# A sample tile's outputs and its 32 state updates moved from behind a chunked scan into it

## What is computed

```python
def gla_block(S, q, k, v, log_a):
    b = jnp.cumsum(log_a, axis=1)
    qf = q * jnp.exp(b); kf = k * jnp.exp(-b)
    inter = jnp.einsum('bchk,bhkv->bchv', qf, S)
    att = tril(jnp.einsum('bihk,bjhk->bhij', qf, kf))
    intra = jnp.einsum('bhij,bjhv->bihv', att, v)
    k_tail = k * jnp.exp(b[:, -1:] - b)
    S_new = S * jnp.exp(b[:, -1])[..., None] + jnp.einsum('bjhk,bjhv->bhkv', k_tail, v)
    return S_new, inter + intra

def gla_output(o, r, g_norm, w_o):
    return (rms_norm(o, g_norm) * silu(r)) @ w_o
```

## Time and profile before

| | |
|---|---|
| median of 3 runs | 2890.35 us |
| the profiled execution | 2889.26 us |
| its span, first to last instruction | 2886.8 us |
| PE busy (share of the span) | 2791.4 us (97%) |
| DVE, ACT, POOL busy | 1168.9, 866.4, 1236.5 us |
| mean granted TensorE clock | 0.989 |

### The profile page before, as it was taken

How to read it: one execution, slowest core, us unless ns; L and a number is a source line. 1 busy time by engine, 2 the same in 40 slices (tenths; PEclk the granted TensorE clock), 3 DMA queues, 4 the chain that set the end, 5 groups by cost and what they waited for, 6 DMA issues and landing times.

```text
span 2886.8 us, 39210 instructions
## 1 busy us (share of the span) xinstructions
PE 2791.4 (97%) x15484; PEld 2420.7 (84%) x15484; DVE 1168.9 (40%) x2079; ACT 866.4 (30%) x1513; POOL 1236.5 (43%) x654
## 2 busy tenths in 40 slices
PE   7999999999999999999999988899999999999997
PEld 7977757799889988997788867777798899989986
DVE  2153156452322233246544178855463322232245
ACT  2053242231222223222211056653141222222221
POOL 1211210343776567634212122133252775677645
PEclk9999999999999999999999999999999999999999
DMA  4111216110210221031444333476111201221021
GB/s 134 52 37 44 91 64 226 37 52 30 59 36 22 58 58 44 15 95 37 128 135 143 123 134 107 168 291 236 44 53 36 55 8 54 58 58 31 27 73 66
DMA packets 197372, 232.26 MB, mean 80 GB/s; under 512 B 8944, under 2 KB 141808, under 8 KB 195200
## 3 DMA queue, kind: packets, MB, share of 16 engines
q1 hardware_dynamic: 197248, 230.54, 24.8%
HBM read 184.90 MB, written 45.61 MB: 80 GB/s over the span
## 4 chain that ended last, share of the span: by engine, by line
PE 44%; DVE 4%; issue 1%; DMA 1%; ACT 1%; POOL 0%; SPq 0%; DVEq 0%; ACTq 0%
PE ps L1480 13%; PE ps L1498 12%; PE ps L1781 8%; PE ps L1668 3%; DVE stats L2513 1%; PE ps L1884 1%; PE ps L1751 1%; PE ps L1847 1%; PE ps L1918 1%; DMA o_scr<-oraw 1%; PE ps L1871 1%; PE ps L1470 1%; DVE stats L2226 1%; PE ps L1962 1%; ACT PR L1360 0%
## 5 line engine op out<-in xcount | busy, mean ns | idle before, releaser
L1480 PE MATMUL ps<-xt,wsplit 128*128 128x384 f32 x5184 | 908.2, 335 | 13.1 <-DVEq L2253 5.0
L1480 PEld LDWEIGHTS ps<-xt,wsplit 128*128 128x128 f32 x5184 | 900.8, 188 | 17.9 <-issue 7.1
L852 POOL TENSOR_TENSOR wsplit<-raw,wsplit 128x1024 fp32r<-128x1024 f32 x144 | 354.7, 2470 | 920.8 <-ACT wsplit L1072 843.1
L1498 PE MATMUL ps<-wsplit,xt 128*128 128x512 f32 x3024 | 707.0, 393 | 0.0
L1498 PEld LDWEIGHTS ps<-wsplit,xt 128*128 128x128 f32 x3024 | 564.8, 189 | 122.0 <-issue 6.5
L1781 PE MATMUL ps<-wsplit,HF 128*128 128x512 f32 x2016 | 468.6, 390 | 0.0
L1781 PEld LDWEIGHTS ps<-wsplit,HF 128*128 128x128 f32 x2016 | 377.3, 188 | 81.6 <-DVE x_res L2359 4.2
L2359 DVE TENSOR_TENSOR x_res<-x_res,ps 128x1024 f32<-128x1024 f32 x168 | 205.2, 1221 | 308.3 <-PE ps L1781 308.3
L2351 DVE TENSOR_SCALAR Hf<-ps 128x384 f32<-128x384 f32 x144 | 80.3, 558 | 499.1 <-PE ps L1480 498.4
L1278 ACT ACTIVATE Hf<-Hf 128x384 f32<-128x384 f32 x144 | 75.9, 527 | 428.1 <-DVE Hf L2351 428.1
L922 POOL TENSOR_TENSOR wsplit<-raw,wsplit 128x1024 fp32r<-128x1024 f32 x36 | 86.0, 2389 | 263.9 <-ACT wsplit L1255 263.9
(11 more groups left out here) (196 smaller groups left out, 2782.8 us busy)
## 6 DMA issues: line engine op xcount, KB each, us to landing
raw<-in_w_up SPq DMA_DIRECT2D x64, 512.0 KB, 5.5
raw<-in_w_down SPq DMA_DIRECT2D x64, 512.0 KB, 3.7
kq_scr<-kqst SPq DMA_DIRECT2D x64, 256.0 KB, 2.8
Kc<-in_cache_k SPq DMA_DIRECT2D x8, 2048.0 KB, 13.3
Vc<-in_cache_v SPq DMA_DIRECT2D x8, 2048.0 KB, 8.8
raw<-in_w_in_a SPq DMA_DIRECT2D x24, 512.0 KB, 3.7
out<-kvs SPq DMA_DIRECT2D x36, 256.0 KB, 2.2
raw<-in_w_kv SPq DMA_DIRECT2D x16, 512.0 KB, 4.4
```

What stands on the lines that cost most here:

```text
L852: nc.gpsimd.tensor_tensor(wsplit[:, slot, 1, :], raw[:, slot, :], wsplit[:, slot, 0, :].bitcast(F32), ALU.subtract).then_inc(lo_done, 1)
L1480: last = nc.tensor.matmul(ps[0:M, b, 0:GW], st, xt[:, c, k, ng * GW:(ng + 1) * GW], start=(k == 0 and i == 0), stop=(k == KT - 1 and i == 2))
L1498: last = nc.tensor.matmul(ps[:, u % 6, :], xt[:, a, 2 * j + k, tok:tok + P], wsplit[:, (g + j) % 4, c, k * 512:(k + 1) * 512], start=(j == ...
```

## The change

The sample tile becomes the third of nine "places" (`SMP = 2`): its transposes, scores, state reads and masked products are issued once, ahead of step 8 (`sample_outputs`). Its 32 state updates, called units, are spread over steps 8 to 31: a unit's product goes into columns 256 to 511 of bank 2 or 3, behind the step's key-value product into the same bank, and DVE updates the stream's state behind S1 or behind S0. Steps 8 to 31 have 1, 1, 2, 1, 1, 2, ... units: 16 steps have one (in bank 2), 8 have two. A copy of the sample tile's values is made on POOL (`vS`). The gate of tile 0 moves to step 8, that of tile 1 behind the last step. The states are written to HBM as their units come; the prompt's final state goes into the buffer of a stream's state that has been written out, and is stored from there.

```diff
+    def units_of(s):
+        behind = max(0, s - FIRST_UNIT)
+        n = SCAN_STEPS - FIRST_UNIT
+        return range(behind * UNITS // n, (behind + 1) * UNITS // n) if s >= FIRST_UNIT else range(0)
...
-        for t in range(2):
-            gates_back(t)
-        sp.wait_ge(state_updated, 2 * PT * H_A)
-        sp.dma_start(gla_prompt[0, 0].rearrange("h k v -> k h v"), S[:, 0]).then_inc(states_out, 16)
-        for t in range(2, 4):
+        for t in range(3):
             gates_back(t)
         for e in range(2):
             for j in range(STREAMS // 2):
-                sp.wait_ge(smp_updated, 4 * (2 * e + 1) + j + 1)
+                sp.wait_ge(smp_updated, 16 * e + 4 * j + 4)
...
+        sp.wait_ge(state_updated, 2 * PT * H_A)
+        sp.dma_start(gla_prompt[0, 0].rearrange("h k v -> k h v"), Ss[1][:, 0]).then_inc(odd_states_out, 16)
+        gates_back(3)
+        sp.wait_ge(scan_out, H_A * TILES)
...
             for c in range(2):
                 if s:
                     pe.wait_ge(state_updated, 2 * (s - 1) + c + 1)
-                nc.tensor.matmul(ps[:, 2 + c, 0:DV], kts[c * CH:(c + 1) * CH, s % 2, :],
-                                 vO[c * CH:(c + 1) * CH, t, h * DV:(h + 1) * DV],
-                                 start=True, stop=True).then_inc(scan_kv, 1)
+                if units_until(s, c):
+                    pe.wait_ge(smp_updated, units_until(s, c))
+                last = nc.tensor.matmul(ps[:, 2 + c, 0:DV], kts[c * CH:(c + 1) * CH, s % 2, :],
+                                        vO[c * CH:(c + 1) * CH, t, h * DV:(h + 1) * DV], start=True, stop=True)
+                for m in units_of(s)[c:c + 1]:
+                    e, j, hs_ = unit(m)
+                    last = nc.tensor.matmul(ps[:, 2 + c, DV:2 * DV], ktb[32 * j:32 * j + 32, e, hs_ * P:(hs_ + 1) * P],
+                                            vS[32 * j:32 * j + 32, hs_ * DV:(hs_ + 1) * DV], start=True, stop=True)
+                last.then_inc(scan_kv, 1)
...
         for s in range(steps):
+            if s == FIRST_UNIT:
+                sample_outputs()
+                pe.wait_ge(smp_blocks, 1)
             if s + 1 < steps:
                 scores(s + 1)
             outputs(s)
...
-        state_products(0, 0)
-        pe.wait_ge(smp_masked, 1)
...
-        state_products(0, 1)
-        state_products(1, 0)
-        state_products(1, 1)
-        pe.wait_ge(smp_updated, 2 * STREAMS)
-        pe.wait_ge(scan_normed, 2 * TILES)
...
+            if (t, half) == (0, 0):
+                pe.wait_ge(keys_by_token, SCAN_STEPS)
+                pe.wait_ge(scores_masked, SCAN_STEPS)
+                pe.wait_ge(state_updated, 2 * SCAN_STEPS)
+                pe.wait_ge(smp_updated, UNITS)
...
+            units = units_of(s)
+            if s == FIRST_UNIT:
+                dve.wait_ge(smp_state_out, 1)
+            for m in units[0:1]:
+                state_unit(m, 2)
             dve.wait_ge(scan_kv, 2 * s + 2)
...
+            to = Ss[1][:, 0, h, :] if t == PT - 1 else S[:, 0, h, :]
+            nc.vector.scalar_tensor_tensor(to, S[:, 1, h, :], elast[:, h, 2 * t + 1:2 * t + 2],
                                            ps[:, 3, 0:DV], ALU.mult, ALU.add).then_inc(state_updated, 1)
+            for m in units[1:2]:
+                state_unit(m, 3)
...
+            if s == FIRST_UNIT:
+                dve.wait_ge(smp_scores, 1)
...
+                gate(0)
...
+                if s == FIRST_UNIT + 2:
+                    normed(2 * SMP)
+                    normed(2 * SMP + 1)
...
-        mean_square(steps // 2 - 1)
-        normed(steps // 2 - 1)
...
-        gate(0)
+        mean_square(pair(steps // 2 - 1))
         gate(1)
```

More of the change, by code:

```diff
@@ L415, in sample_scores, with place_of, tile_at, scan_outs @@
         return ps[:, 2 * (w % 2):2 * (w % 2) + 2, :].rearrange("p a n -> p (a n)")[:, 0:512 + SEQ_S]
+    SMP = 2
+    SCAN_STEPS = PT * H_A
+    FIRST_UNIT = SMP * H_A
+    UNITS = 4 * STREAMS
+    def place_of(t):
+        return SMP if t == PT else t + (t >= SMP)
+    def tile_at(place):
+        return PT if place == SMP else place - (place > SMP)
+    def scan_outs(s):
+        return H_A * place_of(s // H_A) + s % H_A + 1
+    def units_of(s):
+        behind = max(0, s - FIRST_UNIT)
+        n = SCAN_STEPS - FIRST_UNIT
+        return range(behind * UNITS // n, (behind + 1) * UNITS // n) if s >= FIRST_UNIT else range(0)
+    def units_until(s, c):
+        return max([m + 1 for v in range(s) for m in units_of(v)[c:c + 1]], default=0)
+    def unit(m):
+        return m // 16, m // 4 % 4, m % 4
     PRODUCTS = ("k", "k", "q", "q", "v", "v")
@@ L1155, in squares @@
         def squares(p):
-            t, hp = p // 2, p % 2
-            act.wait_ge(scan_out, 4 * t + 2 * hp + 2)
+            place, hp = p // 2, p % 2
+            act.wait_ge(scan_out, 2 * p + 2)
             if p >= 4:
@@ L1173, in _ @@
         for s in range(steps):
+            if s == FIRST_UNIT:
+                act.wait_ge(smp_turned, 4)
+                for e in range(2):
+                    last = nc.scalar.mul(ktb[:, e, :], ps[:, 0, :], cst[:, C_SG + e:C_SG + e + 1])
+                last.then_inc(smp_blocks, 1)
             if s + 2 < steps:
@@ L1177, in _ @@
                 to_tokens(s + 1)
+            if s == FIRST_UNIT:
+                squares(2 * SMP)
+                squares(2 * SMP + 1)
             if s % 2 == 1:
[L1179 to L1194, removed]
+                squares(2 * place_of(s // H_A) + s // 2 % 2)
+        act.wait_ge(scan_out, H_A * TILES)
+        act.wait_ge(smp_updated, UNITS)
+        act.wait_ge(states_out, 16 * STREAMS // 2)
         for grp in range(NG):
@@ L1563, in outputs @@
             t, h = s // H_A, s % H_A
+            place = place_of(t)
             pe.wait_ge(keys_by_token, s + 1)
+            if s == FIRST_UNIT:
+                pe.wait_ge(smp_blocks, 1)
+                pe.wait_ge(smp_q_spread, 4)
             for c in range(2):
@@ L1590, in _ @@
             outputs(s)
[L1593 to L1628, removed]
@@ L1641, in _ @@
[L1641 to L1644 removed]
+        def gated_half(t, half):
+            if (t, half) == (0, 0):
[3 more added lines that the diff above has]
+                pe.wait_ge(smp_updated, UNITS)
+            if (t, half) == (1, 1):
+                pe.wait_ge(scan_normed, 2 * TILES)
```

106 lines of the change are left out of this document (63 added, 43 removed).

## The result

The changed kernel took **2974.17 us** (median of 4 runs, 2943.78 to 2976.41) against 2889.74 us of the kernel before: ratio 1.0265, interval 1.0198 to 1.0333, 2.7% slower. The forecast was 2908, with a range of 2897 to 2916: the direction was right, the size was not. The profiled execution took 2976.41 us, its span is 2974.5 us, the mean granted clock 0.964.

The account below looks back on a forecast made before the run. A DVE loop was taken to pace scan steps at 2.57 us, and DVE the work behind the scan. Terms 7.0 + 28.4 + 0.9 - 17.7 = +18.6 gave 2908 us, range 2897 to 2916.

Parts of the forecast that it names:

- Sample block, +7.0: Ahead of step 8: the sample tile's outputs hold up the scan on PE, 7.0 us more.
- The drain between 64 and 32 rows: In steps 8 to 31: each change of row size drains PE, about 0.62 per product, 3.57 us with one unit.
- the rivals without or with half of it: Unit products in the scan: no drain, 2885 us, 10%; drain only where rows are shared, 2894 us, 8%.
- +28.4 for the units on PE: Steps 8 to 31: drained steps of 3.57 and 4.19 us, 90.1 against 61.7 in all, 28.4 us more.
- DVE in step 10, +0.9: Step 10: the sample tile's norms on top of update and mask make the next S1 late, 0.9 us more.
- Behind the scan, -17.7: From the scan's end to the first output product: that product starts at 448.5 instead of 466.19, 17.7 us less.
- The queue of SP: Writes and reloads on SP: residual tiles start as before, tile 3's gate has 3 us to land, 0 us.

Follow-up runs that it names:

- experiment 7: The changed kernel without the eight second unit products in bank 3, so one unit product a step; 2904.22 us, ratio 1.005.
- experiment 1: The changed kernel without the 32 unit products on PE, all else kept; 2885.81 us, ratio 0.999.
- experiment 6: The kernel before with unread 32-row products in the change's pattern (1, 1, 2 a step) in steps 8 to 31; 2971.91 us, ratio 1.0256.
- (8): The changed kernel with both key-value products of a step first and its one or two units behind them; 2901.86 us, ratio 1.0042.
- (2): The changed kernel with each unit product on the 64 rows of its key-value product instead of 32; 2896.6 us, ratio 1.0029.
- (3): The changed kernel plus six unread products of 384 columns behind each transpose of steps 9 to 31; 2934.31 us, ratio 1.0159.
- experiments 4: The kernel before with one unread 32-row product between the key-value products of steps 8 to 31; 2915.43 us, ratio 1.0094.
- 5: The kernel before with one unread 64-row product between the key-value products of steps 8 to 31; 2896.49 us, ratio 1.0024.

## Why the prediction was wrong in size

- **Sample block, +7.0**: right. 6.7.
- **The drain between 64 and 32 rows**: right, and the rivals without or with half of it fell: in experiment 7, at full clock, steps 9 to 30 take 3.57 or 3.58, step 11 aside, whichever quarter of the rows the unit is on. Gap 0.33 at both places, 0.62 for the unit, 3.57 for the step, as worked out from the earlier trace rows. The Trainium skill, TensorEngine Tiling (Array Packing), section Tiling Modes, that a change of the mode drains the engine, agrees with the 0.33 in the change; the rule of row groups that run concurrently (TensorE: Matmul & The Clock Gate, Part 3) shows here only between equal part sizes, as the last two rows above have it.
- **+28.4 for the units on PE: the step that failed.** It priced 24 steps at the full clock, 90.1 us. They took 155.7, so the term is +94.0. Its first two steps took 3.73 and 3.57; the third, with two units, ran into half the clock, and the rest of the scan stayed there, with steps of 6.48 and 7.63 for the 3.57 and 4.19 of the forecast. I read in the earlier trace rows that the clock falls where PE idles, and took it for granted in a scan in which PE is always busy. But busy, in this column, is not the same as working: a drained product has 0.33 without a load ahead of it, and such products now made up the greater part of a step (four of 0.62 in 3.57, five in 4.19). No rival had the clock in it; one should have. The Trainium skill has a case near this one: TensorE: Matmul & The Clock Gate, Part 1, under "A second HAM failure mode: psum-queue depth-cycling", tells of a kernel whose engine idles so briefly and so often between groups of matmuls that the clock falls back and recovers. The trace agrees in that the clock fell without a long idle time, here with none in PE's record; it differs in that the clock did not come back between steps, but stayed at 0.50 for 157 us.
- **DVE in step 10, +0.9**: cannot be read, since PE's clock halved in that very step, and behind it DVE waited for PE. In experiment 7, where PE drains at full clock, step 10 takes 3.57 and step 11 takes 3.93 (399.00 to 402.93), 0.36 more, since S1 comes late for L1625: there the mechanism held, at less than the forecast's size. Where PE does not drain, DVE's additions cost 4.1 us (experiment 1).
- **Behind the scan, -17.7**: -15.9; 9.0 us lie there where 7.3 were forecast, and it is 9.0 at full clock in the scan too (experiment 1). The gate of tile 2 ends 5.6 behind the scan and not 4.8, since the last norm waits 0.59 for POOL's power, which I had taken as ready; from there to the product it is 3.4 and not 2.4. The mechanism was right.
- **The queue of SP**: right. The gate of tile 3 starts at 548.81 without a wait for its reload. The one wait for a reload, 0.70, is that of the gate of tile 5 at 553.82, and PE does not wait for it. In experiment 1 the gate of tile 3 waits 0.62 for its reload, still ahead of the product, which again does not wait.

What the fall hangs on: the pattern of drained products by itself brings it (experiment 6), taking out every fourth of them (7), putting them side by side (8), or making them undrained (2) prevents it; with dense products between them (3) it falls in two of the eight steps with two units and comes back each time. Before it fell in the change, PE did five products in a row, each drained (two key-value, two units, the masked one), and so it did in experiment 6; in experiments 4 and 7, whose steps have four, it did not fall. More than that these runs do not say. In the change's fourth run, 2943.78 us with a mean clock of 0.975, less time was lost, and the four runs of experiment 6 lie between 2945 and 2988; why the loss differs from run to run is open.

## What to carry to other kernels

Keep matmuls of one part size together: a lone 32-row product between 64-row ones made a step 1.0 us longer where a 64-row one in its place made it 0.2 to 0.3 longer (experiments 4 and 5), and order alone was worth 72 us here. Price a change on TensorE twice, once at each clock level, and ask whether it makes gaps on an engine that already counts as busy; where the answer is unclear, the lower level belongs into the rivals. In the profile, read PEclk and the count of records per stretch before the busy column.

## What the hardware showed that was not expected

- The granted clock fell from 1.00 to 0.50 with no idle time in PE's record, and stayed there for some 157 us (395.4 to about 552.4), until some 2.7 us after the output product's dense matmuls had begun. At that level the gaps doubled, 0.33 to 0.65, and a step took 1.8 times as long, 6.48 for 3.57.

```profile
551.00:552.00 1.00, 1.00 (x3) 0.74 (x3) 0.94 (x2) 0.00 (x0) 0.00 (x0) 0.50 1.03 418
553.00:554.00 1.00, 1.00 (x6) 0.84 (x5) 0.29 (x2) 0.00 (x0) 0.00 (x0) 1.00 0.99 397
```

- More work made a kernel faster: 138 dense products added to the change took 40 us off it, since the clock held for most of the scan and came back each time it fell.
- Two 32-row products next to each other overlap even on the same 32 rows (four loads in 0.72 in experiment 8); one alone between 64-row products waited 0.33 at full clock in every step that was read here.
